# Summing adaLN weight rows on GpSimd out of a shared ring of weight slots, with TensorE adding up by ones

## The reference, cut to what matters

```python
cond = silu(c)                                   # one row of 1024
for l in range(2):
    mod = cond @ w_ada[l] + b_ada[l]             # 6 x 1024 values
    sh1, sc1, g1, sh2, sc2, g2 = split(mod, 6)
    h = rms_norm(x, g_norm_mix[l]) * (1 + sc1) + sh1
    z = h @ w_in[l]                              # 1024 -> 2884
    mix = concat(dsa(z), hgrn2(z), gmlp(z)) @ w_out[l]
    x = x + g1 * mix
    h = rms_norm(x, g_norm_ffn[l]) * (1 + sc2) + sh2
    x = x + g2 * (swiglu(h) if l == 0 else moe_swiglu(h))
```

## Time and profile before

| | us |
|---|---|
| median of 3 runs (lowest, highest) | 2801.14 (2799.39, 2801.37) |
| the profiled execution | 2796.36 |
| its span, first to last instruction | 2794.5 |
| PE busy | 2369.7 |
| DVE busy | 1970.1 |
| ACT busy | 1407.1 |
| POOL busy | 28.0 |

### The profile page before, as it was taken

How to read it: one execution, slowest core, us unless ns; L and a number is a source line. 1 busy time by engine, 2 the same in 40 slices (tenths; PEclk the granted TensorE clock), 3 DMA queues, 4 the chain that set the end, 5 groups by cost and what they waited for, 6 DMA issues and landing times.

```text
span 2794.5 us, 31076 instructions
## 1 busy us (share of the span) xinstructions
PE 2369.7 (85%) x12719; PEld 2011.4 (72%) x12719; DVE 1970.1 (70%) x2343; ACT 1407.1 (50%) x1356; POOL 28.0 (1%) x52
## 2 busy tenths in 40 slices
PE   4936799886477799999999999997658899778898
PEld 4726699765366688888888888886546898656898
DVE  6565754476456688888888888887554788675787
ACT  5322443342423477777767777776324443355432
POOL 0000000000000000000000000000000000000000
PEclk9957899988578799999999999999878999878999
DMA  9400745663014699999999999998321455321453
GB/s 344 140 30 5 271 155 192 202 223 110 6 34 151 251 354 357 354 356 354 357 341 348 359 354 356 355 356 303 102 90 48 142 189 191 109 76 53 148 186 106
DMA packets 293718, 590.71 MB, mean 211 GB/s; under 512 B 11702, under 2 KB 86564, under 8 KB 292928
## 3 DMA queue, kind: packets, MB, share of 16 engines
q1 hardware_dynamic: 289872, 572.33, 58.1%
q0 software_dynamic: 3696, 16.32, 1.9%
HBM read 587.56 MB, written 1.05 MB: 211 GB/s over the span
## 4 chain that ended last, share of the span: by engine, by line
PE 59%; DVE 4%; ACT 2%; DMA 1%; issue 1%; POOL 0%; SPq 0%; DVEq 0%; ACTq 0%
PE ps L1127 18%; PE ps L1129 17%; PE ps L1128 17%; PE ps L1209 1%; PE ps L1333 1%; PE ps L1316 1%; PE ps L1294 1%; PE ps L1194 1%; ACT arena L892 1%; DVE arena L1793 1%; PE ps L1232 1%; DVE arena L1646 1%; PE ps L1166 1%; PE ps L1183 0%; DVE w_lo L1631 0%
## 5 line engine op out<-in xcount | busy, mean ns | idle before, releaser
L792 ACT ACTIVATE w_hi<-raw 128x2048 fp32r<-128x2048 f32 x548 | 1041.7, 1907 | 593.8 <-PE ps L1129 462.6
L1631 DVE TENSOR_TENSOR w_lo<-raw,w_hi 128x2048 fp32r<-128x2048 f32 x548 | 1225.2, 2273 | 56.7 <-ACT w_hi L792 41.1
L1127 PE MATMUL ps<-w_hi,xT_hi 128*128 128x512 f32 (+3 forms) x1600 | 637.1, 398 | 46.3 <-DVE xT_lo L1739 24.7
L1129 PE MATMUL ps<-w_hi,xT_lo 128*128 128x512 f32 (+3 forms) x1600 | 623.5, 390 | 0.0
L1128 PE MATMUL ps<-w_lo,xT_hi 128*128 128x512 f32 (+3 forms) x1600 | 623.0, 389 | 0.0
L1127 PEld LDWEIGHTS ps<-w_hi,xT_hi 128*128 128x128 f32 x1600 | 307.1, 192 | 113.6 <-DVE xT_lo L1739 26.1
L1128 PEld LDWEIGHTS ps<-w_lo,xT_hi 128*128 128x128 f32 x1600 | 307.4, 192 | 61.8 <-issue 3.4
L1129 PEld LDWEIGHTS ps<-w_hi,xT_lo 128*128 128x128 f32 x1600 | 306.4, 191 | 62.3
L1127 PE MATMUL ps<-xT_hi,w_hi 128*128 128x256 f32 x1056 | 299.8, 284 | 4.3 <-DVE xT_lo L1678 4.3
L1129 PE MATMUL ps<-xT_hi,w_lo 128*128 128x256 f32 x1056 | 299.5, 284 | 0.0
L1128 PE MATMUL ps<-xT_lo,w_hi 128*128 128x256 f32 x1056 | 299.5, 284 | 0.0
(11 more groups left out here) (322 smaller groups left out, 1946.0 us busy)
## 6 DMA issues: line engine op xcount, KB each, us to landing
raw<-in_moe_w_gate SPq DMA_DIRECT2D x112, 1024.0 KB, 5.6
raw<-in_moe_w_up SPq DMA_DIRECT2D x112, 1024.0 KB, 5.3
raw<-in_moe_w_down SPq DMA_DIRECT2D x112, 1024.0 KB, 5.4
raw<-in_w_ada SPq DMA_DIRECT2D x48, 1024.0 KB, 5.2
raw<-in_f_w_up SPq DMA_DIRECT2D x44, 1024.0 KB, 5.1
raw<-in_f_w_down SPq DMA_DIRECT2D x22, 1024.0 KB, 5.0
raw<-in_w_in SPq DMA_DIRECT2D x20, 1024.0 KB, 5.8
raw<-in_a_w_in SPq DMA_DIRECT2D x12, 1024.0 KB, 5.3
```

What stands on the lines that cost most here:

```text
L792: act.activation(w_hi[:, k % HI, 0:LEN[k]], raw[:, r, 0:LEN[k]], ACT.Copy).then_inc(w_hi_ready, 1)
L1127: pe.matmul(out_, lh, rh, start=start, stop=False)
L1129: return pe.matmul(out_, ll, rh, start=False, stop=stop)
L1631: dve.tensor_tensor(w_lo[:, k % RAW, 0:LEN[k]], raw[:, k % RAW, 0:LEN[k]], w_hi[:, k % HI, 0:LEN[k]].bitcast(F32), ALU.subtract).then_inc( ...
```

## The change

Only shift and scale of layer 0's first half stay a layer of PE (`ada00`, now 8 slots). The other 40 slots of `w_ada` keep their size and are loaded into the same ring `raw`, but POOL uses them: they stand behind slots of other layers, by `AFTER`, and have their own semaphore of use, `ada_used`. `RING[k]` is the place in the ring of main slot k. Four stand in `in{l}` (gate{l}0, behind its 2nd, 4th, 6th and 8th slot), eight behind the last slot of `in{l}` (shift{l}1), twelve in `ffn0` behind every second slot (gate01, shift10), four behind `out1` (gate11).

For each such slot POOL multiplies it in place by the conditioning column of its partition (2048 columns), adds the halves (1024), and adds the two remaining quarters to a row of sums in arena (512 each), with a wait for itself after each. The bias stands on partition 0 of the sums alone. Later PE multiplies the sums by a matrix of ones (`conditioned`), which adds them over the partitions and puts them on all; ACT copies the result back to arena. The sums use arena during the mixer, where `h_LF` lay; `h_LF` now lies in `mix`. `gate_free` and `shift_free` take the place of `mod_free`.

```diff
-        h_LF = Cut(arena)(768, b=2)
+        h_LF = mix[:, :, 0:BD]
...
             s = {}
             for l in range(2):
-                for half in range(2):
-                    s[f"ada{l}{half}"] = linear_slots(a["w_ada"][l, :, half * 3 * D:(half + 1) * 3 * D], 3 * D)
+                if l == 0:
+                    s["ada00"] = linear_slots(a["w_ada"][0, :, 0:2 * D], 2 * D)
...
-        ORDER = ["ada00", "in0", "out0", "ada01", "ffn0", "ada10", "in1", "out1", "ada11", "over", "moe",
+        ORDER = ["ada00", "in0", "out0", "ffn0", "in1", "out1", "over", "moe",
...
+        AFTER, PARTS = {}, {}
+        pool_slots = []
+        def part(name, l, half, gate, after):
+            c0 = half * 3 * D + (2 * D if gate else 0)
+            slots = linear_slots(a["w_ada"][l, :, c0:c0 + (D if gate else 2 * D)], D if gate else 2 * D)
+            PARTS[name] = len(pool_slots), len(slots)
+            for slot_, k in zip(slots, after):
+                AFTER.setdefault(k, []).append(len(pool_slots))
+                pool_slots.append(slot_)
+        for l in range(2):
+            k = BASE[f"in{l}"]
+            part(f"gate{l}0", l, 0, True, range(k + 1, k + 9, 2))
+            part(f"shift{l}1", l, 1, False, [k + 11] * 8)
+            if l == 0:
+                k = BASE["ffn0"]
+                part("gate01", 0, 1, True, range(k + 1, k + 9, 2))
+                part("shift10", 1, 0, False, range(k + 9, k + 25, 2))
+            else:
+                part("gate11", 1, 1, True, [BASE["out1"] + 3] * 4)
+        RING, RING_POOL, OWNER = [], [], []
+        for k in range(len(LEN)):
+            RING.append(len(OWNER))
+            OWNER.append((w_used, k + 1))
+            for j in AFTER.get(k, ()):
+                RING_POOL.append(len(OWNER))
+                OWNER.append((ada_used, j + 1))
+        def filled(n):
+            return raw_full[n % RAW], 16 * (n // RAW + 1)
...
-            def load(src, nk, nf):
+            def fill(src, nk, nf):
                 nonlocal n
                 r = n % RAW
                 if n >= RAW:
-                    sp.wait_ge(w_used, n - RAW + 1)
+                    user, used = OWNER[n - RAW]
+                    sp.wait_ge(user, used)
+                skipped = n - RING[BASE["moe"]]
+                if 0 <= skipped < RAW:
+                    user, used = OWNER[RING[ROUTED] - RAW + skipped]
+                    sp.wait_ge(user, used)
                 dst = raw[:, r, 0:nk * nf].rearrange("p (k f) -> p k f", k=nk)
                 sp.dma_start(dst, src).then_inc(raw_full[r], 16)
                 n += 1
+            k = 0
+            def load(src, nk, nf):
+                nonlocal k
+                fill(src, nk, nf)
+                for j in AFTER.get(k, ()):
+                    nk, nf, src = pool_slots[j]
+                    fill(src, nk, nf)
+                k += 1
...
-            def ada_bias(l, half):
-                if (l, half) != (0, 0):
-                    pool.wait_ge(mod_free, got(mod_free))
-                load(arena[:, 0:3 * D], a["b_ada"][l, half * 3 * D:(half + 1) * 3 * D].partition_broadcast(P),
-                     ld_mod)
+            load(arena[:, 0:2 * D], a["b_ada"][0, 0:2 * D].partition_broadcast(P), ld_mod)
+            def step(ins):
+                ins.then_inc(pool_step, 1)
+                pool.wait_ge(pool_step, sent(pool_step))
+            def weighted_sums(name, l, half, at, width, free=None):
+                if free is not None:
+                    pool.wait_ge(free, got(free))
+                dst = arena[:, at:at + width]
+                c0 = half * 3 * D + at
+                step(pool.memset(dst, 0.0))
+                load(dst[0:1, :], a["b_ada"][l:l + 1, c0:c0 + width], ld_bias)
+                pool.wait_ge(ld_bias, got(ld_bias, 16))
+                first, count = PARTS[name]
+                for i in range(count):
+                    n = RING_POOL[first + i]
+                    sem, total = filled(n)
+                    pool.wait_ge(sem, total)
+                    w = raw[:, n % RAW, :].rearrange("p (k f) -> p k f", k=4)
+                    o = dst[:, i // 2 * FG:i // 2 * FG + FG]
+                    c = condT[:, i % 2 * 4:i % 2 * 4 + 4]
+                    step(pool.tensor_tensor(w, w, c.unsqueeze(2).to_broadcast([P, 4, FG]), ALU.mult))
+                    step(pool.tensor_tensor(w[:, 0:2, :], w[:, 0:2, :], w[:, 2:4, :], ALU.add))
+                    step(pool.tensor_tensor(o, o, w[:, 0, :], ALU.add))
+                    ins = pool.tensor_tensor(o, o, w[:, 1, :], ALU.add)
+                    ins.then_inc(ada_used, 1)
+                    pool.wait_ge(ada_used, sent(ada_used))
...
+                if l == 0:
+                    pool.wait_ge(cond_ready, got(cond_ready))
+                weighted_sums(f"gate{l}0", l, 0, 2 * D, D, gate_free if l else None)
+                weighted_sums(f"shift{l}1", l, 1, 0, 2 * D, shift_free)
                 if l:
                     pool.wait_ge(lb_free, got(lb_free))
                     load(lb_rows, a["hgrn_lb_logits"].partition_broadcast(P), ld_lb)
                 pool.wait_ge(ws_free, got(ws_free))
                 load(ws, a["gmlp_w_s"][l].rearrange("g t s -> t g s"), ld_ws)
                 load(bs_rows, a["gmlp_b_s"][l], ld_ws)
-                ada_bias(l, 1)
                 gain_row(a["g_norm_ffn"][l])
+                weighted_sums(f"gate{l}1", l, 1, 2 * D, D, gate_free)
+                if l == 0:
+                    weighted_sums("shift10", 1, 0, 0, 2 * D, shift_free)
...
+            def conditioned(at, banks):
+                for i, bank in enumerate(banks):
+                    act.wait_ge(ada_out, got(ada_out))
+                    act.activation(arena[:, at + i * FG:at + i * FG + FG], ps[:, bank, :], ACT.Copy).then_inc(ada_rows, 1)
             for l in range(2):
-                cond_columns()
-                linear(f"ada{l}0")
+                if l == 0:
+                    cond_columns()
+                    linear("ada00")
                 norm()
                 linear(f"in{l}")
                 act.activation(bsT, ps[:, 1, 0:4], ACT.Copy).then_inc(ws_sb, 1)
                 root(stat_b[:, 0:2])
                 to_columns(3)
+                conditioned(2 * D, (4, 5))
                 linear(f"out{l}")
-                cond_columns()
-                linear(f"ada{l}1")
+                conditioned(0, (6, 7, 4, 5))
                 norm()
                 if l == 0:
                     dense("ffn0", False)
+                    conditioned(2 * D, (2, 3))
+                    conditioned(0, (0, 1, 2, 3))
...
+            def conditioned(name, at, banks):
+                first, count = PARTS[name]
+                pe.wait_ge(ada_used, first + count)
+                pe.wait_ge(ada_rows, got(ada_rows, 0))
+                for i, bank in enumerate(banks):
+                    pe.matmul(ps[:, bank, :], ones, arena[:, at + i * FG:at + i * FG + FG],
+                              start=True, stop=True).then_inc(ada_out, 1)
+                got(ada_rows, len(banks))
...
+                if to is main_pass:
+                    conditioned("gate11", 2 * D, (0, 1))
                 down(E_GROUPS - 1)
...
                 to_columns(mix, 3)
+                conditioned(f"gate{l}0", 2 * D, (4, 5))
                 linear(f"out{l}")
-                pe.wait_ge(cond_cols, got(cond_cols))
-                linear(f"ada{l}1", 1, True)
+                conditioned(f"shift{l}1", 0, (6, 7, 4, 5))
                 to_columns(H)
                 if l == 0:
-                    dense()
+                    dense(lambda: conditioned("gate01", 2 * D, (2, 3)))
+                    conditioned("shift10", 0, (0, 1, 2, 3))
...
-            def norm(adaptive):
+            def norm(adaptive, conditioned=0):
                 dve.wait_ge(sumsq_ready, got(sumsq_ready, 2))
                 gains[0] += 16
                 inv_root(rstd, sumsq, D)
                 scale = gain
                 if adaptive:
+                    if conditioned:
+                        dve.wait_ge(ada_rows, got(ada_rows, conditioned))
                     stt(mod[:, 1, :], mod[:, 1, :], 1.0, gain, ALU.add, ALU.mult)
                     scale = mod[:, 1, :]
                 for b in range(TB):
                         tt(H[:, b, :], H[:, b, :], mod[:, 0, :], ALU.add)
                 beat().then_inc(rows_ready, 1)
                 dve.wait_ge(rows_ready, sent(rows_ready))
+                if adaptive:
+                    beat().then_inc(shift_free, 1)
+                    dve.wait_ge(shift_free, sent(shift_free))
...
                 to_columns(3)
+                dve.wait_ge(ada_rows, got(ada_rows, 2))
                 linear(f"out{l}", into_residual(True))
-                beat().then_inc(mod_free, 1)
-                dve.wait_ge(mod_free, sent(mod_free))
-                ada(f"ada{l}1")
+                beat().then_inc(gate_free, 1)
+                dve.wait_ge(gate_free, sent(gate_free))
```

53 lines of the change are left out of this document (33 added, 20 removed).

## The result

On the same chip the changed kernel takes **2853.28 us** (median; 2840.94 to 2861.82) against 2801.26 before: a ratio of 1.0187, 95% interval 1.0159 to 1.0216, slower by 52 us. The prediction was 2883 with slower as the likeliest side.

A forecast was written before the change was run, and what follows sets the result against it. DVE's timeline was taken to show the stages, with PE waiting for DVE in norms and mixers. 2796.4 - 129.7 + 7 + 72.4 = 2746; turns' +132 gave 2878, and 4.8 more 2883 us; range 2735 to 2915.

The forecast's parts named there:

- ropes: Mixers: DVE's 26 rope and copy instructions take turns with POOL's 12 instructions, 29.7 us a layer, +59 in both.
- ffn0: Feed-forward: DVE and POOL in turns need 15.0 us per two slots against 11.3, 12 times, +43.
- ring wait: Before in0's and in1's last evacuation: DVE's early out splits wait for POOL's slots, 4T - 3.5 = 36 us each, +72.
- norms: Norms of ffn0, in1 and the experts: five two-input DVE instructions meet POOL's gate steps, four turns each, +30.
- Turns: Two-input DVE instructions wait for the POOL instruction in progress, alternating; +132 at full price, 2883 us; chance 0.57.
- T: POOL's time for one slot's four instructions over 4096 columns: taken as 9.9 us, low end 4.9.
- layers removed, passes and gain row in their place: Conditioning layers: removal takes off 129.7 us; PE's passes, possible ACT copies and in1's gain row add 7.
- S0: First of eight POOL slots between in0's last slot and out0: loadable once in0_7 is used (124.1), landing at 129.3.
- S5 to S7: Last three of the eight POOL slots ahead of out0: 12 instructions beside the ropes, each a turn, 3T = 29.7 us.
- They don't meet: Rival: POOL has its own way into SBUF, DVE's splits and ropes keep their times; 2751 us, chance 0.33.
- T = 13: Rival: POOL much slower, without turns; mixer waits 2 x 48.5, ffn0 20 more; 2796 us, no change, chance 0.06.
- Half the turns: Rival: long POOL passes are met only where DVE has nothing to wait for; 2817 us, within turns' 0.57.

The follow-up runs named there:

- e4: Changed kernel without the weighted sums: POOL only waits for each slot, writes one column and gives it back; 2722.29 us, ratio 0.9713.
- e3: Changed kernel with each tensor_tensor of POOL's sums replaced by two memsets of the same size, which write but don't read; 2746.18 us, ratio 0.9823.
- e10: e7 with every instruction of POOL's sums cut to 512 columns; 2751.22 us, ratio 0.9830.
- e13: e10 with the load of lb_rows issued behind the fifth slot of shift11's sums instead of the eighth; 2737.50 us, ratio 0.9771.
- e12: Changed kernel with shift01, shift11 on PE, three gates behind norms, every third feed-forward slot followed by POOL's, gate11's slots behind ada11's; 2760.92 us, 0.9854.
- e1: Changed kernel with ACT's and DVE's early out-layer splits moved to just ahead of the wait for o_out; 2833.66 us, ratio 1.0115.
- e7: Changed kernel with late out splits, shift01 and shift11 sums behind ropes, three gates behind norms, POOL slot behind every third feed-forward slot; 2757.29 us, 0.9864.

## Why the prediction was right, and where it was off

**Right**: the side, by the mechanism it gave. The size, 2883, is 30 us too high: ropes and ffn0 were priced 37 us too high together, and ring wait, norms and router 9 too low. Turns are taken, 8.9 us a slot against T = 9.9, and the mixers wait for the ring with ACT w_hi as releaser, in both layers. By its steps, predicted and found:

| Step | predicted | found |
|---|---|---|
| layers removed, passes and gain row in their place | -123 | -123.4 in the gaps |
| ring wait, two layers | +72 | +74.8 |
| ropes and copies | +59 | +45.1 |
| ffn0 | +43 | +20.4 |
| norms | +30 | +33.5 |
| router, gate11 | 0 (3) | +2.8 |

- **The removal** held. DVE lost 3 us of it at the start, since ada00's last two splits already met POOL (7.90 us for both instead of 4.5).
- **The ring wait** was right in size, in part by luck, and only half right in cause. S0's start, predicted for 129.3 and found at 129.29, agrees by chance. In the changed kernel everything in in0 comes 4.2 us earlier (the fifth evacuation at 130.75 instead of 134.99), and so did S0's slot, which had landed at 125.07. POOL was late: its gate sums were stretched by in0's splits, and its memset (122.27) and the wait of 4.38 us for its bias row came behind them. That is +4.2 against the evacuations. Four slots took 37.1 us instead of 39.6, which is -2.5, so 38.0 was found in layer 0 for 36.1 predicted. And the formula, 4T - 3.5, falls to nothing as T does; e4, with T near 0, still waits 20.2. What failed is "S0 can be loaded once in0_7 is used" as the only load counted: S5 cannot be issued before in0's last slot is used, and the transfers behind it land one after another (2.7 us apart in e4). In after, POOL's chain is the longer one: from S4's start at 166.40 it is 9.4 us to the evacuation (9.3 predicted). The low end of 16 each was too low.
- **"S5 to S7 are 12 POOL instructions, each a turn: 3T = 29.7"** was too much by 7 a layer: a DVE instruction that waits runs inside the turn, so twelve of the 24 rope instructions come free. 3 x 8.86 plus the twelve left at 0.33, 4.0, is 30.6; 176.89 to 207.37 is 30.5.
- **ffn0 is the term that was mis-sized**: "per two slots DVE holds 2 x 2.29 and about half an us of its act_low, POOL 9.9: 15.0". Adding both held times takes for granted that they never find a gap. POOL's slots follow every 12.7 us, DVE busy 101.5 of 143. The right bound is POOL's pace against the ring's 11.3: (12.7 - 11.3) x 12 = 17, and e3 puts the sums at 16.6 (4 more are loads). The sign "a group near 22 us" was too high; 20 was found.
- **The norms**: priced about right each (6.2 to 10.1 against 9.9), but four of them, not three: gate00's first slots land during the first norm.
- **Two signs were off.** POOL was busy for 466.3 us, not 350 to 400: 40 slots of 8.86 are 354, and the waits inside instructions count as busy. Its product of 2048 columns takes 3.60 us alone, not 4 to 5.
- **The rivals.** "They don't meet" is shown false by e3 against after: ratios of 0.9823 and 1.0187, some 100 us, of which about 10 go to the shorter slot of e3 and the rest to reading. "T = 13" is false, T is 8.9. "Half the turns" comes nearest in its time, and is no better a description: each turn met is paid in full, fewer are met.
- The condition was too narrow. "An instruction with two SBUF inputs" misses copies, casts and tensor_scalar within SBUF: in e3 they wait for memsets. The same class makes nearly all of the router's +2.8: a CAST of 0.17 us that is issued inside POOL's sum of 1024 columns and ends 0.03 after it (+1.4), and a tensor_scalar that takes 1.31 us instead of 0.23 (+1.1):

```profile
963.55 1.54 DVE L2290 CAST small<-small 128x8 f32<-128x8 uint32 x1
...
966.46 1.31 DVE L1769 TENSOR_SCALAR small<-const,small 128x8 f32<-128x8 f32 x1
```

```profile
962.72 2.34 POOL L805 TENSOR_TENSOR raw<-raw 128x1024 f32<-128x1024 f32 x1
```

The Trainium skill ("SBUF — State Buffer", Who interferes with whom) has both conditions: two SBUF inputs contend with a GpSimd instruction that reads, and copy, cast and tensor_scalar in a two-port mode with any. The runs agree: 1.29 and 2.99 us in e3. Its figure in "GPSIMD Engine Reference" (Performance versus the Vector engine), 4497 ns for 2048 columns with two inputs, fits the sum of two full inputs (2.34 for 1024) and not the product here, 3.60, whose second input is a broadcast column.

**Open**: the rest of the program, from the memset on, took 1870 to 1885 us from run to run with the same code. In the traces it goes with TensorE's granted clock: the lower of its two levels (1.2 GHz of 2.4) was granted there for 213 us in after, 226 in e10, 238 in e13 and 257 in e12, whose rests took 1871.9, 1874.1, 1882.8 and 1885.5. Why it was granted for longer in some runs is open, and differences under 10 us between the experiments' spans should not be read without the table of stretches. Ahead of the memset the lower level was granted for 328 us before and 454 after; what that costs in the single stretches was not measured apart from the waits.

## What to carry to other kernels

- Work given to an idle engine is paid where it meets another: first ask which instructions of the two exclude each other, then give it the stretches in which the other idles or reads PSUM. With the same 40 slots the program takes 52 us more than the kernel before, or 63 less (e13), by where the sums start, how long one instruction is, and what stands behind them in the queues.
- In a ring that is filled in order, a slot of a slow user delays every slot behind it; an early split ahead of an evacuation turns that into a wait of the whole chain. Look ahead only as far as the slots of the same user reach, and look what else the slow engine's queue holds: a row load behind the sums made DVE wait 27 us longer.
- An expected gain that comes from removing a wait needs a second look at what the wait kept apart (e1).

## What the hardware showed unexpectedly

A short DVE instruction in turns costs DVE up to one whole POOL instruction and POOL next to nothing (3.63 instead of 3.60 us), while a split of 2.29 us costs POOL most of its length: a product of 3.60 takes 5.54, a sum of 2.34 takes 4.34 in ffn0. In e7 all 32 MAX8 and 32 MATCH_REPLACE8 of the mixers stand beside POOL's sums and keep their 0.28 to 0.43 us; so do the instructions with one input in PSUM (0.69 us for 512 columns throughout). And cutting POOL's instructions to 512 columns costs 1.0 us a slot (9.83 against 8.86) but takes 5 of 8 us out of a norm in the mean.
